# Strassen's scheme for the dense layer of a two-block network, all 1024 rows at once

## What is computed

```python
def _swiglu(h, w_gate, w_up, w_down):
    return (jax.nn.silu(h @ w_gate) * (h @ w_up)) @ w_down
...
        h = _rmsnorm(x, ffn_norm[l])
        if l % 2 == 0:
            j = l // 2
            x = x + _swiglu(h, dense_w_gate[j], dense_w_up[j], dense_w_down[j])
```

## Time and profile before

| | us |
|---|---|
| median of three runs | 5590.12 |
| profiled execution: span | 5587.1 |
| dense layer, first transfer to next stage's first transfer | 1817.81 to 2589.24 |
| TensorE busy, whole span | 5157.5 |
| VectorE / ScalarE / GpSimd busy | 2743.0 / 2225.6 / 342.1 |

### The profile page before, as it was taken

One profiled execution on the slowest core, in us unless ns is written; L12 is line 12 of the kernel. 1 busy time (PEld: TensorE's weight loads), 2 busy tenths in 40 slices (PEclk: granted clock), 3 DMA queues, 4 the chain that ended last, 5 costly groups with the idle time before them and its releaser, 6 DMA issues. The chain is left out here.

```text
span 5587.1 us, 97211 instructions
## 1 busy us (share of the span) xinstructions
PE 5157.5 (92%) x38308; PEld 4523.6 (81%) x38309; DVE 2743.0 (49%) x4394; ACT 2225.6 (40%) x3437; POOL 342.1 (6%) x564
## 2 busy tenths in 40 slices
PE   7986989899899999997989988999999999999994
PEld 5675967677677899996867678989898999999994
DVE  2597545333834555554156434444444554555444
ACT  2454236333443444443234423333334444444432
POOL 0111100000600000000023001000000000000001
PEclk8997999999999999998999999999999999999997
DMA  2110010310003655553100425444444555555444
GB/s 88 35 66 17 0 37 1 134 51 30 8 12 123 244 209 205 191 208 115 46 16 19 139 113 185 155 157 158 164 158 175 184 195 186 194 196 188 181 157 188
DMA packets 104610, 688.52 MB, mean 123 GB/s; under 512 B 12320, under 2 KB 16304, under 8 KB 63280
## 3 DMA queue, kind: packets, MB, share of 16 engines
q1 hardware_dynamic: 90752, 639.74, 31.6%
q0 software_dynamic: 8816, 27.44, 1.3%
q10 hardware_dynamic: 4800, 17.83, 0.8%
HBM read 622.67 MB, written 62.29 MB: 123 GB/s over the span
## 5 line engine op out<-in xcount | busy, mean ns | idle before, releaser
L3374 DVE TENSOR_TENSOR experts_low<-experts_raw,experts_high 128x1024 fp32r<-128x1024 f32 x678 | 810.5, 1223 | 982.9 <-ACT experts_high L3301 982.9
L3236 PE MATMUL ps<-experts_xs_high,experts_high 128*128 128x256 f32 (+1 forms) x3584 | 1036.1, 289 | 39.0 <-issue 36.7
L3236 PE MATMUL ps<-experts_xs_low,experts_high 128*128 128x256 f32 (+1 forms) x3584 | 1034.3, 289 | 0.0
L3236 PE MATMUL ps<-experts_xs_high,experts_low 128*128 128x256 f32 (+1 forms) x3584 | 1034.3, 289 | 0.0
L3236 PEld LDWEIGHTS ps<-experts_xs_high,experts_high 128*128 128x128 f32 x3584 | 679.3, 190 | 50.5 <-issue 42.4
L3301 ACT ACTIVATE experts_high<-experts_raw 128x1024 fp32r<-128x1024 f32 x678 | 687.8, 1050 | 40.9 <-DMA experts_raw<-experts 40.9
L3236 PEld LDWEIGHTS ps<-experts_xs_low,experts_high 128*128 128x128 f32 x3584 | 679.4, 190 | 8.1
L3236 PEld LDWEIGHTS ps<-experts_xs_high,experts_low 128*128 128x128 f32 x3584 | 679.1, 189 | 0.4 <-issue 0.4
L2913 PE MATMUL ps<-dense_xs_parts,dense_high 128*128 128x256 f32 x2816 | 499.6, 280 | 7.0 <-DVE dense_low L3022 5.9
L2913 PEld LDWEIGHTS ps<-dense_xs_parts,dense_high 128*128 128x128 f32 x2816 | 437.0, 189 | 14.2 <-issue 7.8
L3228 PE MATMUL ps<-experts_high,experts_hid_high 128*128 128x512 f32 x1120 | 438.5, 392 | 0.0
(11 more groups left out here) (538 smaller groups left out, 9096.3 us busy)
## 6 DMA issues: line engine op xcount, KB each, us to landing
experts_raw<-experts SPq DMA_DIRECT2D x226, 1536.0 KB, 6.4
...
mixT<-w_in SPq DMA_DIRECT2D x36, 512.0 KB, 3.3
...
out_proj_raw<-w_out SPq DMA_DIRECT2D x48, 256.0 KB, 2.8
proj_keys_raw<-w_in SPq DMA_DIRECT2D x20, 512.0 KB, 3.2
x_mixed<-mixT SPq DMA_DIRECT2D x16, 512.0 KB, 2.6
h_rows<-out_proj_rows SPq DMA_DIRECT2D x16, 512.0 KB, 2.6
```

What stands on the lines that cost most here:

```text
L3236: last = nc.tensor.matmul(ps[:, m, 0:width], w[:, u, m, c], x[:, k, 0:width], start=(k == 0 and i == 0), stop=(k == KD - 1 and i == 2))
L3374: nc.vector.tensor_tensor(low[:, v, t, :], raw[:, v % NR, t, :], high[:, v, t, :].bitcast(F32), ALU.subtract).then_inc(split, 1)
```

## The change

`swiglu_passes` is replaced for the dense layer by `winograd_ffn`. It takes all 1024 rows at once and writes both matrix products as products of quarters, by the form of Strassen's scheme that needs seven products of quarters and sums of quarters.

**First half.** The rows are read once and turned by four groups of 16 transposes (`turn`); VectorE makes four sums of quarters of `h` (each 128x2048), and ScalarE and VectorE split the seven operands of the scheme (`xc`). The hidden channels are taken in 11 pairs of 128 (`NF`), and each for gate and then for up: 22 groups (`M`), numbered `mi`. In a group SP loads the four quarters of weights (128x2048, 1 MB), GpSimd makes four differences of them (`weight_sums`, 128x512 each), ScalarE and VectorE split the seven operands (`high`, `low`), and TensorE makes seven products of 4 x 3 matmuls of 512 columns; three of them are added in PSUM to a bank that holds an earlier one. ScalarE copies the first product, VectorE adds up the others, and after both groups of a pair there are four quarters of the hidden values (`hid`). GpSimd makes four sums of these (`hidden_sums`) and issues their stores; SP stores three quarters as they are. All seven go to DRAM (`hid_sums`).

**Second half.** 77 steps: seven products, each over 11 blocks of hidden channels. For a step SP loads a 128x512 hidden operand and a 128x512 weight operand (256 KB each) into one of four slots, ScalarE rounds both in one operation, VectorE makes the low parts, and TensorE makes 4 x 3 matmuls of 512 columns into one of two halves of PSUM. After a product, at its successor's second step, a half of PSUM is folded into the result: `p0`, `u2`, `u3` and `res` are 128x2048 pieces in SBUF. The residual is loaded into `res` by eight transfers in the last group of the first half. The output is written in eight tiles.

**Elsewhere.** The four differences of the down weights are made by GpSimd in the attention stage `mla0` and stored (`quarters`, 11 loads and 11 stores of 1 MB, 44 sums of 128x512). The weights are laid out in quarters on the host. The code of the layer is written out in full, without register loops.

The core of the diff:

```diff
+            @block.sync
+            def _(sp):
+                for f in range(NF + 1):
+                    if f < NF:
+                        if f >= 2:
+                            sp.wait_ge(summed, 4 * (f - 1))
+                        sp.dma_start(quarter[:, f % 2], of[:, f]).then_inc(fetched[f % 2], 16)
+                    if f:
+                        sp.wait_ge(summed, 4 * f)
+                        sp.dma_start(to[:, f - 1], sums[:, (f - 1) % 2]).then_inc(kept[(f - 1) % 2], 16)
...
+            @block.gpsimd
+            def _(pool):
+                for f in range(NF):
+                    r, s = quarter[:, f % 2], sums[:, f % 2]
+                    pool.wait_ge(fetched[f % 2], 16 * (f // 2 + 1))
+                    if f >= 2:
+                        pool.wait_ge(kept[f % 2], 16 * (f // 2))
+                    nc.gpsimd.tensor_tensor(s[:, 0, :], r[:, 1, :], r[:, 0, :], ALU.subtract).then_inc(summed, 1)
+                    pool.wait_ge(summed, 4 * f + 1)
+                    nc.gpsimd.tensor_tensor(s[:, 1, :], r[:, 3, :], s[:, 0, :], ALU.subtract).then_inc(summed, 1)
+                    nc.gpsimd.tensor_tensor(s[:, 2, :], r[:, 3, :], r[:, 1, :], ALU.subtract).then_inc(summed, 1)
+                    pool.wait_ge(summed, 4 * f + 2)
+                    nc.gpsimd.tensor_tensor(s[:, 3, :], r[:, 2, :], s[:, 1, :], ALU.subtract).then_inc(summed, 1)
...
+def winograd_ffn(core, name, NF, w_in, w_down, w_sums, h_sums, residual, out):
...
+    STEPS = 7 * NF
...
+    BANK = (0, 1, 2, 3, 0, 2, 3)
+    SOURCE = (("raw", 0), ("sum", 1), ("sum", 2), ("sum", 0), ("raw", 2), ("sum", 3), ("raw", 3))
...
+    GROUP = (0, 1, 0, 1, 0, 1, 0)
+    ORDER2 = (0, 1, 4, 2, 3, 5, 6)
...
+            for b in range(NT):
+                to = rows_a[:, b, :] if b < 4 else rows_b[:, b - 4, :]
+                sp.dma_start(to, d["h_rows"][b * P:(b + 1) * P, :]).then_inc(rows_in[b], 16)
...
+            fetch(0)
+            fetch(1)
...
+            def fetch_step(n):
+                i, f = ORDER2[n // NF], n % NF
+                kind, q = SOURCE[i]
+                sp.dma_start(step_raw[:, n % 4, 0, :], h_sums[H_ROW[i]][:, f, :]).then_inc(step_in[n % 4], 16)
+                sp.dma_start(step_raw[:, n % 4, 1, :], (w_down if kind == "raw" else w_sums)[:, f, q, :]).then_inc(step_in[n % 4], 16)
...
+            for mi in range(M):
+                if mi + 2 < M:
+                    sp.wait_ge(split, 7 * (mi + 1))
+                    fetch(mi + 2)
+                if mi == M - 1:
+                    sp.wait_ge(product, 7 * mi + 1)
+                    for r in range(3):
+                        sp.wait_ge(h_stored[r], 16 * (NF - 1))
+                    for n in range(4):
+                        fetch_step(n)
+                    sp.wait_ge(product, 7 * mi + 5)
+                    for b in range(NT):
+                        sp.dma_start(res[:, b, :], residual[b * P:(b + 1) * P, :]).then_inc(res_in, 16)
...
+            for n in range(4, STEPS):
+                sp.wait_ge(step_split, n - 3)
+                if n == NF - 1:
+                    for r in range(3):
+                        sp.wait_ge(h_stored[r], 16 * NF)
+                if n == NF:
+                    sp.wait_ge(s_stored, 64 * NF)
+                fetch_step(n)
+            for b in (4, 5, 6, 7):
...
+            def weight_sums(mi):
+                r = raw[:, mi % 2]
+                pool.wait_ge(loaded[mi % 2], 16 * (mi // 2 + 1))
+                def one(to, a, b, after, i):
+                    if mi:
+                        pool.wait_ge(split, 7 * (mi - 1) + i + 1)
+                    if after:
+                        pool.wait_ge(summed, 4 * mi + after)
+                    nc.gpsimd.tensor_tensor(sums[:, to, :], a, b, ALU.subtract).then_inc(summed, 1)
...
+            def hidden_sums(f):
+                def one(to, a, b, op, made, after):
+                    pool.wait_ge(h_made, 4 * f + made)
...
+                    nc.gpsimd.tensor_tensor(hs[:, to, :], a, b, op).then_inc(h_summed, 1)
+                one(0, hid[:, H21, :], hid[:, H22, :], ALU.add, 3, 0)
+                one(1, hs[:, 0, :], hid[:, H11, :], ALU.subtract, 3, 1)
+                one(2, hid[:, H11, :], hid[:, H21, :], ALU.subtract, 3, 0)
+                one(3, hid[:, H12, :], hs[:, 1, :], ALU.subtract, 4, 2)
+                for n in range(4):
+                    pool.wait_ge(h_summed, 4 * f + n + 1)
+                    pool.dma_start(h_sums[3 + n][:, f, :], hs[:, n, :]).then_inc(s_stored, 16)
...
+            for mi in range(M):
+                if mi + 1 < M:
+                    weight_sums(mi + 1)
+                if mi % 2 == 0 and mi:
+                    hidden_sums(mi // 2 - 1)
...
+            turn(1, rows_a, 0)
+            for b in range(4, NT):
+                pe.wait_ge(rows_in[b], 16)
+            turn(0, rows_b, 0)
+            pe.wait_ge(x_copied, 1)
+            turn(1, rows_b, 1)
+            for mi in range(M):
+                for i in range(7):
+                    q = 7 * mi + i
...
+                        if i == 3:
+                            pe.wait_ge(x_split, 4)
+                            turn(1, rows_a, 1)
+                        pe.wait_ge(x_split, X_READY[i])
...
+                    pe.wait_ge(split, q + 1)
...
+                    if i == 4:
+                        pe.wait_ge(first_kept, mi + 1)
+                    if i == 5:
+                        pe.wait_ge(u_made, 3 * mi + 2)
+                    if i == 6:
+                        pe.wait_ge(u_made, 3 * mi + 3)
+                    bank = ps[:, 4 * (mi % 2) + BANK[i], :]
+                    for k in range(4):
+                        c = slice(k * P, (k + 1) * P)
+                        for t, (w, x) in enumerate(((0, 0), (0, 1), (1, 0))):
+                            last = nc.tensor.matmul(bank, wc[:, i, w, c], xc[i][:, x, k, :], start=i < 4 and k == 0 and t == 0,
+                                                    stop=k == 3 and t == 2,
+                                                    skip_group_check=i >= 4)
...
+            for n in range(STEPS):
+                o, f = divmod(n, NF)
+                i = ORDER2[o]
+                pe.wait_ge(step_split, n + 1)
...
+                if o >= 2 and f == 0:
+                    pe.wait_ge(kept, o - 1)
+                for a in range(4):
+                    for t, (x, w) in enumerate(((step_high, step_high), (step_high, step_low), (step_low, step_high))):
+                        last = nc.tensor.matmul(ps[:, 4 * GROUP[o] + a, :], x[:, n % 4, 0, a * P:(a + 1) * P], w[:, n % 4, 1, :],
+                                                start=i < 4 and f == 0 and t == 0, stop=f == NF - 1 and t == 2, skip_group_check=i >= 4)
+                    if n == STEPS - 1 and a < 3:
+                        last.then_inc(tile_done, 1)
+                last.then_inc(step_done, 1)
...
+            def high(mi, i):
+                q = 7 * mi + i
+                if mi:
+                    act.wait_ge(product, q - 6)
...
+                copy(wc[:, i, 0, :], weights_of(mi, i), ACT.Copy).then_inc(rounded, 1)
+            def high_step(n):
+                act.wait_ge(step_in[n % 4], 32 * (n // 4 + 1))
+                if n >= 4:
+                    act.wait_ge(step_done, n - 3)
...
+                copy(step_high[:, n % 4], step_raw[:, n % 4], ACT.Copy).then_inc(step_rounded, 1)
...
+            act.wait_ge(turned, 1)
+            copy(a11[:, :, :], group(1), ACT.Copy).then_inc(x_copied, 1)
+            act.wait_ge(x_copied, 1)
+            copy(x_high(0), a11[:, :, :], ACT.Copy).then_inc(x_rounded, 1)
+            high(0, 0)
+            act.wait_ge(x_summed, 2)
+            copy(x_high(1), s2[:, :, :], ACT.Copy).then_inc(x_rounded, 1)
+            high(0, 1)
+            copy(x_high(2), x_sum(2), ACT.Copy).then_inc(x_rounded, 1)
...
+            for mi in range(M):
+                f, gate = mi // 2, mi % 2 == 0
+                base = 4 * (mi % 2)
+                for i in range(7):
+                    if i == 0:
+                        act.wait_ge(product, 7 * mi + 1)
+                        if mi:
...
+                        copy(acc[:, 0, :], ps[:, base, :], ACT.Copy).then_inc(first_kept, 1)
...
+                        copy(hid[:, tile, :], source, ACT.Silu).then_inc(silu_done, 1)
+                    if mi + 1 < M:
+                        high(mi + 1, i)
+                    elif i >= 3:
+                        high_step(i - 3)
+            for n in range(4, STEPS):
+                if n == NF + 1:
+                    act.wait_ge(step_done, NF)
+                    copy(flat(p0), flat(group(0)), ACT.Copy).then_inc(kept, 1)
+                high_step(n)
...
+            def low(mi, i):
+                q = 7 * mi + i
+                dve.wait_ge(rounded, q + 1)
+                tt(wc[:, i, 1, :], weights_of(mi, i), f32(wc[:, i, 0, :]), ALU.subtract).then_inc(split, 1)
...
+            low_x(1, 0, a11[:, :, :])
```

(65 more changed lines are left out.)

477 lines of the change are left out of this document (201 added, 276 removed).

## The result

| | before | after |
|---|---|---|
| median of the runs, us | 5590.1 (4 runs, 5587.6 to 5602.16) | 5527.07 (4 runs, 5525.15 to 5529.61) |
| ratio of the runs | | 0.9886, 95% interval 0.9872 to 0.99 |
| profiled execution: time, span | span 5587.1 | 5528.34, span 5522.1 |

The changed kernel is 63 us faster by the medians and 65.0 by the spans; forecast were 65.1 and 5525.0 us. The sum came out right, but not term by term: the price of a column and the lead-in were each put about 6 us too high, and a cost of the second half that the sum did not have made up for most of it.

The account below looks back on a forecast made before the run. The prediction took TensorE's matmul stream, counted in columns, to bound the dense layer. Its terms -104.2 - 7.7 + 28.7 + 0 + 5 + 13 - 0.9 + 1 sum to -65.1, from 5590.1 to 5525.0 us, range 5508 to 5556.

Parts of the forecast that it names:

- Columns: TensorE's matmuls in the layer: 2772 of 512 columns at 0.229 us, 634.8 against 739.0, so -104.2 us.
- Transposes out of the stream: Dense layer: 64 transposes leave TensorE's matmul stream for the lead-in, -7.7 us.
- Lead-in: Layer's start: first matmul at 25 us, first group ends at 63.5; 44.3 instead of 15.6, +28.7 us, bounds +24 to +34.
- Steady first half, 0: Groups of the first half: other engines' work and waits stay covered by TensorE's 19.2 us per group; 0, at most +15.
- Before step 4, +5: Start of second half: residual loads queued ahead delay the step's operands; +5 us, bounds 0 and +9.
- E + 14.3 against E + 11: E: end of first half's last group; step 4's low part ready at E + 14.3, TensorE wants it at E + 11.
- Folds, +13: Second half, second steps of products 2 to 7: copy and adds delay low parts; +13 us, bounds 11 and 16.
- End, -0.9: Layer's end: last matmul to next stage takes 7.1 us instead of 8.0, -0.9.
- Attention, +1: Attention before the layer: GpSimd's 44 sums may disturb VectorE's 32 scalings; +1 us, bounds 0 and 42.
- The scalings on the path: Rival, attention: each of 32 scalings waits one whole GpSimd sum, +42 in place of +1, 5566 us; chance 0.08.
- GpSimd's pace: Rival, first half: GpSimd's sums beside VectorE need 21.2 us per group, +44, 5569 us; chance 0.07.
- The starving steps: Rival, second half: slow transfers starve TensorE above 7.9 us landing; at 12, +79, 5604 us, slower than before; chance 0.07.

Follow-up runs that it names:

- Experiment 1: Changed kernel with the eighth product given back, by repeating matmuls in both halves: 5607.5 us, ratio 1.0023 to the kernel before.
- the repeat: Changed kernel run once more with nothing edited: 5525.8 us, ratio 0.9886 to the kernel before.
- Experiment 4: Changed kernel, group 0's first-product copy and two adds moved earlier: 5520.9 us; third add moved too, with folds and residual edits: 5495.0 us.
- Experiment 6: Changed kernel with GpSimd making each of a group's four weight differences twice: 5534.0 us in one run.
- experiment 3: Changed kernel with the eight residual loads spread over every second step from the seventh on: 5515.9 us, ratio 0.9865 to the kernel before.
- experiment 2: Changed kernel with the folds at the fourth step of the next product instead of the second: 5508.2 us, ratio 0.9847 to the kernel before.
- experiment 8: Changed kernel with memsets in place of the attention's 44 GpSimd differences: execution 5572.6 us; attention stage to layer 216.0 us, with sums 216.2 and 215.7.
- experiment 7: Changed kernel with a third 256 KB transfer in every second-half step from the fifth on: 5519.6 us in one run.

## Why the prediction was right, and where not

**Columns, right; the price was 1% high.** 2772 matmuls at 0.2267 are 628.4, not 634.8. I had taken 0.229 from ten starts at the end of the layer; over 1764 matmuls of a busy stretch it is 0.2267. -6.4. Experiment 1 confirms the term that carries the gain: 396 matmuls more made the layer 89.7 us longer, 0.2266 each.

**Transposes out of the stream**: as forecast, they stand in the lead-in.

**Lead-in, mis-sized.** The step said that the first matmul starts at 25 us and the second group at 63.5. Measured were 22.8 and 57.4 (23.3 and 57.8 in the repeat), so 38.3 us stand ahead of the layer's stream of columns, not 44.3: -6.0. The fifth product started at 47.5 where I had 50.8, so about half of the error was made before it. The wait of the fifth product for ScalarE's copy is there (3.09 us, after 3.59 for a low part behind the fourth turn). But I let TensorE wait again for the adds before the sixth and for what the seventh needs; it did not, because that one pause hid both. Experiment 4 uncovered them one by one.

**Steady first half, 0**: right. Experiment 6 shows how much room there was: GpSimd at 170 of 200 us changed no group.

**Before step 4, +5**: 5.47, and its cause is shown by experiment 3. The size was partly luck: the times that I gave, E + 14.3 against E + 11, make 3.3, the rest was an allowance for GpSimd's stores, and the eight profiles that keep the burst have 4.9 to 7.3. **Folds, +13**: 12.05 (1.45, 0.80, 0.80, 3.00, 3.00, 3.00 where I had 1.6, 0.9, 0.9 and 3.2 three times), shown by experiment 2.

**The half clock in the second half was missing, +7.9, and 0.3 at each of the seven pauses, +2.1; together +10.0.** I had counted it in the lead-in, behind pauses of 4 to 6 us, from the earlier trace rows, and not asked whether a pause of 3 would do the same. It does: with the folds at the second step eight profiles have 24 pauses of 3.0 us, and behind 23 of them the clock stands at 0.50 for a while; behind the 24 of 0.8 and 1.45 us it never does; behind the pause of 4.9 to 7.3 us before the fifth step it always does. The one of 3.0 us without it, in the repeat, has 132 matmuls in 30.22 us behind it, where the same pause of the first profile has 31.67. The Trainium skill (TensorE: Matmul & The Clock Gate, Part 1, on the clock gate) says that the lower clock is the default and that activity releases it; the rows behind the pauses agree, those of the mixing layer show a fall in the midst of activity that this does not explain.

**End, -0.9**: 6.6 us from the last matmul's place in the stream to the next stage, where I had 7.1 and the kernel before 8.0. **Attention, +1**: about 0.5 in this pair of profiles; experiment 8 shows that it is small, but profiles of equal code differ by as much, so its size is not shown. The Trainium skill (SBUF — State Buffer, section Who interferes with whom) says that VectorE's `tensor_scalar` and GpSimd's work can lock each other out of the ports that they share, for a whole instruction; the trace agrees as far as the scalings went from 0.52 to 0.73 us on average and one of 640 columns from 0.55 to 1.67, but of the 42 us that it would have cost had every scaling waited for a whole sum on the path, about 0.5 were paid, since TensorE had work of other units.

The layer adds up: 628.4 + 38.3 + 17.5 + 10.0 + 6.6 = 700.8. By the forecast's terms it was 704.2: -6.4 - 6.0 - 0.5 (pauses) + 10.0 - 0.5 (end) = -3.4. Behind the layer came +5.0 of chance, and by the spans the total met the forecast to 0.1 us (by the medians to 2.1). That is luck: with the 1.1 us by which my check had missed the layer before (770.3 for 771.4) and 0.5 of the attention, errors of 15 us on one side met 15 on the other, inside the range of 5508 to 5556.

**The rivals.** The scalings on the path: out (experiment 8). GpSimd's pace: out for the steady half (experiment 6), with something left of it in the lead-in. The starving steps: out (experiment 7); pieces landed in 3.0 to 3.8 us, where it would have taken 7.9 to starve TensorE, and even 768 KB per step, landing in 3.8 to 4.8, did not slow the steps.

**Left open.** What lets the clock fall in a busy stretch of the mixing layer in ten executions of thirteen. And what decides at which clock the lead-in's 32 transposes run: in five profiles of the new arrangement they took 3.7 us and the layer's first matmul came at 22.6 to 23.3 us, in six they took 5.3 to 5.8 and it came at 24.1 to 25.3.
